# Updating only half of the columns in the levels of a delta-rule inverse and of HGRN2 scores

## The reference, cut to what matters

```python
# gated DeltaNet: a unit lower triangular system of 64 x 64 per chunk and head
kk  = einsum('bhld,bhmd->bhlm', kc, kc)
lhs = eye + where(strict, kk * dec * bc[..., :, None], 0.0)
sol = triangular_solve(lhs, rhs, lower=True, unit_diagonal=True)
# HGRN2: scores with a decay of its own for every channel c
g   = cumsum(fc, axis=2)
dec = _masked_exp(g[:, :, :, None, :] - g[:, :, None, :, :], incl)
a   = einsum('bhlc,bhmc,bhlmc->bhlm', qc, kc, dec)
```

## Time and profile before

| | |
|---|---|
| median of 3 runs | 1228.4 us |
| span of the profiled execution, first to last instruction | 1221.8 us |
| PE busy | 1152.6 us (94%) |
| PEld busy | 1079.3 us (88%) |
| DVE busy | 576.0 us (47%) |
| ACT busy | 396.9 us (32%) |
| mean granted clock of PE | 0.969 of full speed |

### The profile page before, as it was taken

How to read it: one execution, slowest core, us unless ns; L and a number is a source line. 1 busy time by engine, 2 the same in 40 slices (tenths; PEclk the granted TensorE clock), 3 DMA queues, 4 the chain that set the end, 5 groups by cost and what they waited for, 6 DMA issues and landing times. The chain is left out here.

```text
span 1221.8 us, 26871 instructions
## 1 busy us (share of the span) xinstructions
PE 1152.6 (94%) x11789; PEld 1079.3 (88%) x11789; DVE 576.0 (47%) x1035; ACT 396.9 (32%) x546; POOL 11.9 (1%) x29
## 2 busy tenths in 40 slices
PE   5889989998989989999999999789999999999997
PEld 3689978887568889999999989689999999999996
DVE  1657877777578644423333354442222222453332
ACT  2635576521113238522222211242232222331121
POOL 0001100000000000000000000000000000000000
PEclk9789999998699999999999999899999999999998
DMA  9915411113855152453333232213232322232301
GB/s 308 276 47 116 114 36 37 37 37 106 231 168 160 36 131 72 70 138 87 87 86 87 87 86 70 69 35 103 69 103 69 103 69 82 71 95 72 95 1 74
DMA packets 191034, 116.76 MB, mean 96 GB/s; under 512 B 36651, under 2 KB 189352, under 8 KB 190679
## 3 DMA queue, kind: packets, MB, share of 16 engines
q1 hardware_dynamic: 190358, 115.16, 34.1%
q0 software_dynamic: 576, 0.14, 0.1%
HBM read 108.31 MB, written 6.96 MB: 94 GB/s over the span
## 5 line engine op out<-in xcount | busy, mean ns | idle before, releaser
L856 PE MATMUL ps<-high_parts,scr_parts 128*128 128x272 f32 x2848 | 548.6, 292 | 12.8 <-DVE hT_parts L2821 7.0
L856 PEld LDWEIGHTS ps<-high_parts,scr_parts 128*128 128x128 f32 x2848 | 451.6, 189 | 16.8 <-issue 8.3
L856 PE MATMUL ps<-hT_parts,scr_parts 128*128 128x272 f32 x1488 | 412.7, 290 | 0.0
L2718 DVE TENSOR_TENSOR scr_parts<-ring,scr_parts 128x1024 fp32r<-128x1024 f32 (+1 forms) x104 | 133.7, 1286 | 329.1 <-ACT scr_parts L1880 326.4
L856 PEld LDWEIGHTS ps<-hT_parts,scr_parts 128*128 128x128 f32 x1488 | 275.2, 189 | 0.0
L1880 ACT ACTIVATE scr_parts<-ring 128x1024 fp32r<-128x1024 f32 (+1 forms) x104 | 115.2, 1108 | 463.4 <-PE ps L856 457.8
L856 PE MATMUL ps<-pj_parts,scr_parts 128*128 128x272 f32 x992 | 166.5, 292 | 2.1 <-DVEq L2020 1.8
L856 PEld LDWEIGHTS ps<-pj_parts,scr_parts 128*128 128x128 f32 x992 | 140.5, 188 | 3.6 <-DVEq L2020 2.2
L856 PE MATMUL ps<-high_parts,ring_parts 128*128 128x272 f32 x416 | 123.7, 297 | 0.0
L856 PEld LDWEIGHTS ps<-high_parts,ring_parts 128*128 128x128 f32 x416 | 82.5, 198 | 0.1
L856 PE MATMUL ps<-scr 64*64 64x64 f32 (+6 forms) x2352 | 80.1, 233 | 2.7 <-DVEq L2020 1.7
(11 more groups left out here) (332 smaller groups left out, 1181.2 us busy)
## 6 DMA issues: line engine op xcount, KB each, us to landing
ring<-in_w_in_dram SPq DMA_DIRECT2D x62, 512.0 KB, 5.4
ring<-in_ffn_w_in_dram SPq DMA_DIRECT2D x44, 512.0 KB, 5.1
ring<-in_ada_w_dram SPq DMA_DIRECT2D x40, 512.0 KB, 6.7
ring<-in_ffn_w_out_dram SPq DMA_DIRECT2D x16, 384.0 KB, 3.6
ring<-in_ffn_w_out_dram SPq DMA_DIRECT2D x16, 320.0 KB, 4.1
pj<-in_ada_w_dram SPq DMA_DIRECT2D x8, 512.0 KB, 8.2
ring<-in_w_out_dram SPq DMA_DIRECT2D x8, 512.0 KB, 6.2
x_scratch<-scr SPq DMA_DIRECT2D x1, 2176.0 KB, 12.0
```

The source lines that it names most:

```text
L856: return pe.matmul(out, lhsT, rhs, start=start, stop=stop, skip_group_check=True)
L2718: dve.tensor_tensor(lo, src, hi.bitcast(F32), SUB).then_inc(w_split, 1)
```

## The change

A helper takes, out of every 2s columns, the lower s or the upper s. It is applied to the moving operand and to the output of the matmuls of `g_y{n}` and `h_qk{n}`, and to the operands of the two subtractions of `g_upd{n}`. The weights of the matmuls, their number, their order and all semaphores stay as they are, and so do the cost tables, so that the fixed order is the same. On PE 480 matmuls change from 64 columns to 32 (per pair 4 x 32 + 16 of the inverse and 6 x 16 of HGRN2); on DVE 18 subtractions change from 512 columns to 256 (10 on line 2432, 8 on line 2438). The samples (t = 4) keep full columns. For s = 1 the columns of a half lie one by one with a gap of one between them, for s = 32 in runs of 32.

```diff
+def level_half(b, n, upper):
+
+    s = LEVELS[n]
+    return b.rearrange("m (x i) -> m x i", i=2 * s)[:, :, upper * s:upper * s + s]
...
                         if n != levels_of(t)[-1]:
                             for h in range(8):
                                 for r in blocks:
-                                    mm(B0_[r, h * DK:(h + 1) * DK], U_[r, h, :], X_[r, h, :])
+                                    mm(level_half(B0_[r, h * DK:(h + 1) * DK], n, 0), U_[r, h, :], level_half(X_[r, h, :], n, 0))
                         for h in range(8):
                             for r in blocks:
-                                last = mm(B1_[r, h * DK:(h + 1) * DK], X_[r, h, :], U_[r, h, :])
+                                last = mm(level_half(B1_[r, h * DK:(h + 1) * DK], n, 1), X_[r, h, :], level_half(U_[r, h, :], n, 1))
...
-            def pair_scores(keys, queries):
-
+            def pair_scores(keys, queries, n=None):
+
+                cut = (lambda x: x) if n is None else lambda x: level_half(x, n, 1)
...
-                                last = mm(ps[half(b), 6 + q, h * DK:(h + 1) * DK], keys[half(q), p, r], queries[half(q), p, r])
+                                last = mm(cut(ps[half(b), 6 + q, h * DK:(h + 1) * DK]), keys[half(q), p, r], cut(queries[half(q), p, r]))
...
-                        pair_scores(f(hQK), f(hQK)).then_inc(hgrn_s, 1)
+                        pair_scores(f(hQK), f(hQK), n).then_inc(hgrn_s, 1)
...
-                        dve.tensor_tensor(gU, gU, ps[:, 5, :], SUB)
+                        dve.tensor_tensor(level_half(gU, n, 1), level_half(gU, n, 1), level_half(ps[:, 5, :], n, 1), SUB)
...
-                            dve.tensor_tensor(gT, gT, ps[:, 4, :], SUB)
+                            dve.tensor_tensor(level_half(gT, n, 0), level_half(gT, n, 0), level_half(ps[:, 4, :], n, 0), SUB)
```

## The result

Over 20 runs each the changed kernel takes 1234.9 us (1224.5 to 1243.3) and the kernel before 1228.5 us (1224.4 to 1233.6). The ratio is 1.004, 95% interval 1.0022 to 1.0058. It compares runs within 1.5% of the fastest of their kernel; since long runs are part of the effect here, medians over all runs say more. The forecast was 1227.4 us with a range up to 1231.5: the time is outside, on the side of a rival that had 12 in 100. The profiled execution took 1229.2 us with a span of 1227.3 us, so it was one of the shorter ones, and 1.9 us lie around the span. The kernel before had a span of 1221.8 us in its profile; with the same 1.9 us that was about 1223.7 us, just under the shortest of its 20 runs, so both profiles show short executions. Compared matmul by matmul, the changed kernel's profile is 2.2 us behind at 205 us already, ahead of all changed code, and 5.5 us at the end.

The account below looks back on a forecast made before the run. PE's pace through its fixed order was taken as the bound. Matmuls counted 0 and shorter DVE waits 0.20 + 0.53 + 0.27 = 1.0 us, so 1228.4 - 1.0 = 1227.4 us, range 1223.5 to 1231.5.

Parts of the forecast that it names:

- a rival that had 12 in 100: Clock, second pair: fewer columns could bring another half-clock stretch, 1229.1 us with one, 1230.8 us with two; 12 in 100.
- the bounds: On the 480 matmuls, costed at no change: at most 0.3 us gained, or 9.2 us more if strided columns cost four.
- The waits for DVE: Second pair and samples: PE had five, 2.5 us together; halved subtractions were to win 1.0 us of them.
- the one behind level 4: Second pair, PE's 1.17 us wait before the last level's `g_x`: 0.53 us won, 0.64 us left.
- the sum of 1.0 us: PE waits won in the second pair: 0.20 us at level 2, 0.53 at level 4, 0.27 at the last level.
- The rival of strided outputs: `g_y` and `h_qk`, both pairs: strides slow PE, 1236.6 us for all runs, 1229.7 for short ones; 7 and 6 in 100.
- the term for the clock: Second pair: no clock loss in the sum; as rival one or two more half-clock stretches, at most 1.7 us each, 12 in 100.
- what hides the saved columns is the weight load: All 480 matmuls: weight loads set PE's step, about 30 ns, so halving columns changes PE's time by 0.

Follow-up runs that it names:

- run 2: Kernel before with the 18 DVE subtractions halved and the changed matmuls on strided operands with all 64 columns: 1229.2 us.
- run 6: Kernel before with the DVE subtractions halved and the matmuls of 4 moving columns streaming these 8 times (4 in `m_out`): 1225.0 us.
- run 1: Kernel before with only the 18 DVE subtractions halved, all matmuls with full columns: 1229.5 us.
- run 4: Kernel before with the matmuls of 4 moving columns streaming these 8 times (4 in `m_out`), nothing else: 1225.3 us.
- run 12: Kernel before with only the matmuls of 9 moving columns repeating these 8 times, to 72 columns: 1221.0 us.
- run 9: The changed kernel itself measured once more, on a third chip: 1234.0 us, its kernel before at 1230.1 us.
- run 3: Kernel before with only the delta-rule inverse halved, on PE (288 matmuls) and DVE; HGRN2 scores keep 64 columns: 1232.9 us.
- run 7: Kernel before with only the 192 matmuls of the HGRN2 scores halved; inverse and DVE unchanged: 1231.9 us.
- run 10: Changed kernel with all 480 changed matmuls streaming 4 columns instead of 32, rest of their products left out: 1239.1 us.
- run 8: Kernel before with DVE subtractions halved and the matmuls of 4 and of 9 moving columns repeating these (9 become 72): 1218.0 us.

## Why the prediction was wrong

**Right.** The 480 matmuls cost PE what they cost before, with no price for the strides (I had counted records of the earlier trace rows as matmuls, so there are 960 to price, and the bounds were half of what they should have been; at a price of 0 it changes nothing). The subtractions take 0.42 us. The waits for DVE fell, the one behind level 4 to 0.64 us in runs 2 and 6, as forecast. Whether the sum of 1.0 us is exact, the times cannot say: runs 1 and 2 lie 1.0 and 1.2 us under the line (standard errors 0.6 and 0.5), but runs 4 and 12, with full DVE operations, lie 0.8 under it too. The profiles of runs 4 and 6 give 1.4 us for the second pair, so the size was about right. The rival of strided outputs was not there.

**Wrong.** The step that failed is the term for the clock. In the sum it stood at 0; as a rival it was too small: "One costs at most half of 3.4 us, 1.7 us [...]; two give 1230.8 us", and the reason against it, that "4 columns are far fewer than 32, and the changed matmuls stand among others that stay". What the runs show in its place is 12.4 us more at half clock per run, between three and four stretches of 3.4 us and not one or two, at 0.42 us for each us (1.4 us a stretch, where I had 1.7): +5.2 us against the -0.7 us of the rest. The reason did not hold: 480 matmuls of 32 columns among others that stay were enough (run 9), by the clock the 288 of the inverse alone (run 3). Two errors made it small. First, I asked whether the change could bring one more fall in the one stretch that was at 1.00, the second pair, and did not ask how many. They do come there (3.4 us in the first profile of the change, 20.9 in the second; but run 1, with full columns, has 10.2 there, so single profiles do not prove the place), and they come as well between 285 and 345 us, where the clock was 0.80 already and of which I showed no row (0.74 and 0.78). Secondly, I took the places of the falls in one execution for those of the kernel. The kernel before runs between 68 and 111 us at half clock by itself, and its profile was one of the low ones.

The sentence "what hides the saved columns is the weight load" was true and still misled. A saved column that is hidden has no value in time. It has one for the clock, and there it counts against the change: removing hidden columns lost 4 us (run 9 with the 20 runs of the result), adding hidden columns won 4 us (run 4) and 9 us (run 12).

What stays open: which of the changed stages brings how much (run 3 against 7 rests on the clock alone), why runs 3 and 10 lie 2 to 3 us under the line, and what decides in which place the clock falls in a given execution.

## What to carry to other kernels

Where small matmuls are bound by their weight loads, fewer moving columns save nothing on PE and can cost clock; look at the granted clock of each stretch and at its spread over many runs before cutting them. Where a stretch at half clock follows matmuls with very few moving columns, repeat these columns into unused PSUM columns as long as the weight load hides them. A difference under 1% in a program with such stretches is split into time at half clock and the rest, from the span and clock of every run.

## What the runs showed of the hardware

- PE can be busy 3.40 of 3.40 us by the trace, with 3.34 us of weight loads, and the clock falls to 0.50 behind it (415.4 to 418.8 us after; also the earlier trace rows). The Trainium skill, TensorE: Matmul & The Clock Gate, section HAM oscillation, tells of idle gaps as what brings the lower clock; in this case these two rows show a fall without idle, and PE's busy time does not decide alone either: from 317.4 to 334.5 us PE is busy for 16.29 us at 0.50 before and, with the repeated columns of run 8, for 15.98 us at 1.00.
- A repeat costs next to nothing: 64 records with 4 or 16 columns take 2.03 and 2.04 us, 8 with 9 or 72 columns 1.03 and 1.08 us.
- A pattern with gaps, single columns included, costs a 64 x 64 matmul nothing when read from SBUF and written to PSUM (29.6 ns between starts with 64 columns, 29.1 with 32; single columns 14.5 over four quarters, contiguous ones 15.4), and runs of 2 to 32 elements cost DVE nothing when it reads PSUM (0.42 us for 256 elements, as from SBUF in the earlier trace rows).
- The kernel before takes 1221.6 to 1240.4 us over its 105 runs, and the mean granted clock of the run explains the spans of the 85 for which it is known within 1.4 us.
